# The 512-column products of a two-block network take their columns in a reversed, alternating order

## What is computed

```python
proj = jnp.einsum('btd,de->bte', hn, w_in)                # first block: q, k, v, gate
gate, up = jnp.split(jnp.einsum('btd,de->bte', hn, w_in), 2, axis=-1)
... = jnp.einsum('btf,fd->btd', jax.nn.silu(gate) * up, w_out)
gate = jax.nn.sigmoid(jnp.einsum('btd,de->bte', rmsnorm(h, ple_norm[i]), ple_w_gate[i]))
proj = jnp.einsum('bsd,de->bse', h, w_in[l])              # second block
br_a = jnp.einsum('bsc,cd->bsd', y_a, w_proj_mlstm[l])
out = jnp.einsum('bsd,de->bse', merged, w_out[l])
```

## Time and profile before

| | us |
|---|---|
| median of 3 runs | 2201.73 |
| lowest, highest | 2200.83, 2202.91 |
| profiled execution | 2200.2 |
| its span, first to last instruction | 2198.5 |
| PE busy | 2188.7 |
| DVE busy | 1574.8 |
| ACT busy | 1082.1 |

### The profile page before, as it was taken

One profiled execution on the slowest core, in us unless ns is written; L12 is line 12 of the kernel. 1 busy time (PEld: TensorE's weight loads), 2 busy tenths in 40 slices (PEclk: granted clock), 3 DMA queues, 4 the chain that ended last, 5 costly groups with the idle time before them and its releaser, 6 DMA issues.

```text
span 2198.5 us, 27733 instructions
## 1 busy us (share of the span) xinstructions
PE 2188.7 (100%) x9954; PEld 1819.9 (83%) x9954; DVE 1574.8 (72%) x2395; ACT 1082.1 (49%) x1369; POOL 19.8 (1%) x41
## 2 busy tenths in 40 slices
PE   9999999999999999999999999999999999999998
PEld 8888888888888888888888888888888888888887
DVE  6887888877776457777778846889455559645875
ACT  5564554544444334444446545555445555443443
POOL 0000000000000000000000000000000000000000
PEclk9999999999999999999999999999999999999999
DMA  9654566666666666666666656666665556666663
GB/s 281 182 163 122 179 196 189 200 192 195 194 193 192 192 195 191 196 191 194 186 217 198 200 152 191 183 199 181 201 176 171 171 162 205 196 195 211 191 192 114
DMA packets 282925, 413.96 MB, mean 188 GB/s; under 512 B 21071, under 2 KB 145883, under 8 KB 282299
## 3 DMA queue, kind: packets, MB, share of 16 engines
q1 hardware_dynamic: 281806, 408.55, 61.9%
q10 hardware_dynamic: 1008, 3.94, 0.5%
HBM read 410.33 MB, written 2.10 MB: 188 GB/s over the span
## 4 chain that ended last, share of the span: by engine, by line
PE 99%; issue 0%; DMA 0%; DVE 0%; ACT 0%; DVEq 0%; POOLq 0%; POOL 0%; SPq 0%; ACTq 0%
PE acc L1314 31%; PE acc L1316 31%; PE acc L1315 31%; PE mx L1494 1%; PE mx L1535 0%; PE tp L1362 0%; DMA H<-in_x 0%; PE tp L1508 0%; PE tp L1507 0%; PE tp L1509 0%; PE mx L1291 0%; PE mx L1293 0%; PE mx L1292 0%; PE mx L1472 0%; PE tp L1552 0%
## 5 line engine op out<-in xcount | busy, mean ns | idle before, releaser
L1686 DVE TENSOR_TENSOR w_lo<-raw,w_hi 128x1024 fp32r<-128x1024 f32 (+1 forms) x769 | 934.9, 1219 | 524.5 <-ACT w_hi L801 520.7
L801 ACT CAST w_hi<-raw 128x1024 fp32r<-128x1024 f32 (+1 forms) x769 | 803.0, 1046 | 913.9 <-PE acc L1316 897.0
L1314 PE MATMUL acc<-w_hi,xa_hi 128*128 128x512 f32 x2228 | 874.8, 393 | 0.0
L1316 PE MATMUL acc<-w_hi,xa_lo 128*128 128x512 f32 x2228 | 867.4, 389 | 0.0
L1315 PE MATMUL acc<-w_lo,xa_hi 128*128 128x512 f32 x2228 | 867.2, 389 | 0.0
L1316 PEld LDWEIGHTS acc<-w_hi,xa_lo 128*128 128x128 f32 x2228 | 418.2, 188 | 87.8
L1314 PEld LDWEIGHTS acc<-w_hi,xa_hi 128*128 128x128 f32 x2228 | 418.5, 188 | 84.8
L1315 PEld LDWEIGHTS acc<-w_lo,xa_hi 128*128 128x128 f32 x2228 | 418.6, 188 | 84.2
L1314 PE MATMUL acc<-w_hi,xb_hi 128*128 128x512 f32 x384 | 149.6, 390 | 0.0
L1316 PE MATMUL acc<-w_hi,xb_lo 128*128 128x512 f32 x384 | 149.4, 389 | 0.0
L1315 PE MATMUL acc<-w_lo,xb_hi 128*128 128x512 f32 x384 | 149.4, 389 | 0.0
(11 more groups left out here) (313 smaller groups left out, 1240.4 us busy)
## 6 DMA issues: line engine op xcount, KB each, us to landing
raw<-in_w_in SPq DMA_DIRECT2D x192, 512.0 KB, 3.8
raw<-in_ffn_w_in SPq DMA_DIRECT2D x352, 256.0 KB, 2.9
raw<-in_gla_w_in SPq DMA_DIRECT2D x95, 512.0 KB, 4.0
raw<-in_ffn_w_out SPq DMA_DIRECT2D x88, 512.0 KB, 3.7
raw<-in_w_in SPq DMA_DIRECT2D x128, 256.0 KB, 3.0
raw<-in_gla_w_out SPq DMA_DIRECT2D x32, 512.0 KB, 4.1
raw<-in_ple_w_gate SPq DMA_DIRECT2D x32, 512.0 KB, 4.0
raw<-in_w_proj_mlstm SPq DMA_DIRECT2D x32, 512.0 KB, 3.7
```

The source lines that it names most:

```text
L801: nc.scalar.copy(w_hi[:, hl, 0:kc * job.w], raw[:, slot, 0:kc * job.w]).then_inc(hi_ready, 1)
L1314: nc.tensor.matmul(a[t][:, 0:w], xh, hi, start=first, stop=False)
L1316: ins = nc.tensor.matmul(a[t][:, 0:w], xl, hi, start=False, stop=last)
L1686: nc.vector.tensor_tensor(w_lo[:, hl, 0:kc * job.w], raw[:, slot, 0:kc * job.w], w_hi[:, hl, 0:kc * job.w].bitcast(F32), ALU.subtract) \
```

## The change

The three matmuls of `product` take rearranged views of their moving operand and of their output. The new helper splits the 512 columns into two halves h of 32 blocks b of eight columns c, and goes through them with b from last to first outermost, then the two halves, then c from last to first. The opening granules (`opening_product`), the narrow products, the embedding product and the job `pool` keep their views.

```diff
                     for t in range(2) if only is None else (only,):
                         xh = xt_part(job, 0, k)[:, t * P:(t + 1) * P]
                         xl = xt_part(job, 1, k)[:, t * P:(t + 1) * P]
-                        nc.tensor.matmul(a[t][:, 0:w], xh, hi, start=first, stop=False)
-                        nc.tensor.matmul(a[t][:, 0:w], xh, lo, start=False, stop=False)
-                        ins = nc.tensor.matmul(a[t][:, 0:w], xl, hi, start=False, stop=last)
+                        to, high, low = streamed(a[t][:, 0:w]), streamed(hi), streamed(lo)
+                        nc.tensor.matmul(to, xh, high, start=first, stop=False)
+                        nc.tensor.matmul(to, xh, low, start=False, stop=False)
+                        ins = nc.tensor.matmul(to, xl, high, start=False, stop=last)
                     if kk == kc - 1 and only != 0:
                         ins.then_inc(consumed, 1)
                     elif last and only == 0:
                         ins.then_inc(half_done, 1)
+
+            def streamed(tile):
+
+                return tile.rearrange("p (h b c) -> p b h c", h=2, c=8)[:, ::-1, :, ::-1]
```

## The result

The changed kernel takes 2419.41 us (median of 4 runs, 2418.88 to 2421.15) against 2201.28 us for the kernel before; the ratio is 1.0991, 95% interval 1.0972 to 1.1011. It is slower by 218.1 us, 24.0 ns for each of the 9084 changed matmuls. The forecast was no change; the measured time lies in the span of rival A (2270 to 2443 us), near its upper end.

The account below looks back on a forecast made before the run. PE was taken to bound the kernel throughout; instructions 0 plus stream 0 left profiled execution at 2200.2 us, and 1.5 us for the median gave 2201.7 us. Likeliest range 2197 to 2206 us, eight in ten 2197 to 2443 us.

Parts of the forecast that it names:

- rival A: Inside each of the 9084 matmuls, every run change costs a little at full pace: +68 to +241 us, 2270 to 2443 us; chance 0.17.
- The bound: PE busy in 100% of the span, waiting only 2.6 us, so a slower matmul costs its whole increase; 9084 matmuls at 226.7 ns.
- Part (1): Instructions on all queues: none added, removed or moved, no wait, semaphore or transfer changed; cost 0.
- part (2): Column streaming in the changed matmuls: bounds from -134 to +1926 us, 0 taken from the nearest earlier row.
- the row at l = 8: Gated scores, F32, ascending runs of eight alternating between two planes: 101 ns a matmul, no penalty seen; nearest evidence for 0.
- l = 1: Gated scores with read and output stepping by two columns: eight matmuls in 0.82 us against 0.81, taken as no cost.
- l = 2: Gated scores in alternating runs of two columns: 0.87 us against 0.81 for eight matmuls, 7.5 ns per 128 columns.
- 0.117 ns per run: Possible price of each run change in a changed matmul, from the scores' runs of two: 7.5 ns a matmul, +68 us.
- l = 4: Gated scores in alternating runs of four columns: 0.81 us for eight matmuls, no cost where a price per run predicted 0.03 us.
- Rival B: Changed matmuls' stream falls to half rate through descending pairs or broken output: +1926 us, 4128 us; chance 0.17.
- Rival C: A gain in the changed matmuls as their time beside streaming shrinks: down to 2068 us at the utmost; chance 0.03.
- the 14.7 ns beside the streaming: Part of each changed matmul's 226.7 ns pace beyond 212 ns for 512 columns; its whole removal would give -134 us.

## Why the prediction was wrong

**The bound** was read rightly. PE sets the time throughout, nothing is hidden, and 9084 times the change of pace is the result: +24.0 ns gave +218 us. The other way it is so only in the main: 9120 x -10.9 ns is -99 us, of which 89 came, since PE then waits a little for DVE.

**Part (1)** held: the instruction counts are equal, the clock's row stayed, and the unchanged groups kept their durations but for the 36 opening products. The dearest group of these has a mean of 457 ns instead of 417, but 417 in the kernel that only reads in the new order and takes the same time, so this isn't the order's doing, and it is under 2 us in all.

**The failed step is the choice of 0 in part (2)**: the row at l = 8 of the earlier trace rows, ascending and at 0.828 ns a column, was taken for the changed matmuls at 0.414 ns a column. The prediction had named this limit ("a penalty that brings a column from 0.414 up to 0.828 ns could hide there") and then chosen by likeness of shape. The alternating ascending kernel is that very shape at the full pace, and costs 16.4 ns a matmul, (212 + 16.4) / 512 = 0.446 ns a column: far below 0.828. That such a price hides under the slow pace of an F32 pass fits the read at a step of two: nothing in the F32 rows (l = 1), and 451 ns in F32R, (451 - 14.7) / 512 = 0.852 ns a column. But it stays an argument, and one row speaks against it: alternating runs of two did show at l = 2, though in F32R they have a pace of 333 ns, (333 - 14.7) / 512 = 0.62 ns a column, also below 0.828. Shown is that the row at l = 8 doesn't carry over to the full pace; why isn't. The second half of the choice, that a reversed run touches the same words and is free, failed too: 6.5 ns for the plain reversal, and 9 ns of duration for the descending blocks on top of the alternation (416 against 407).

**Rival A** has the place (inside each matmul, PE's other groups unchanged) and, by its upper bound of 26.5 ns, nearly the size, but not the mechanism: neither of its prices describes the rows. 0.117 ns per run gives 3.7 ns for runs of sixteen, which cost 13.2. One column's time per run does give 13.2 ns there (32 x 0.414), but 53 ns for runs of four, which cost 23.2, and 26.5 ns for 64 runs, which cost 16.4 when they alternate in ascending order and 6.4 when the blocks go backwards over the whole tile. That its bound lay close to 24.0 ns is chance. I had given it 0.17 because l = 4 and l = 8 showed nothing at the slow pace.

**Rival B** is out: the moving operand's descending order costs 6.5 ns, not 212, and the output's order nothing. The sentence weighed there, that "any non-contiguous AP slows matmuls significantly" (the Trainium skill, PSUM — Partial Sum Buffer, Specifications), doesn't hold for this output: 2200.44 against 2200.31 us. For the read, the Trainium skill's Advanced Engine Details and Errata (SBUF Cachelines) has full performance as long as at least two accesses hit a 16-byte line. The runs here disagree both ways: each run of eight fills two such lines, and the alternating kernel is 6.8% slower all the same; two columns in turn, 256 apart, never hit a line twice in a row, and are faster than plain order.

**Rival C**, a gain from the 14.7 ns beside the streaming, didn't come with this order, and I was wrong that nothing could touch them: with two columns in turn the pace is 215.8 ns, 10.9 of the 14.7 gone.

**What stays open** is the mechanism of the fetch. Shown is: it is the read of the moving operand; it costs from some run length between 32 and 64 columns downwards when far halves alternate; the distance is of little weight; no DMA and no work of ACT or DVE beside it is needed for the price; any reversal or block order of 4, 8 or 16 columns over the whole tile costs the same 6 to 7 ns; swapping neighbouring blocks of eight, ascending inside, costs much more, 43 ns of duration. That the read alone matters is shown for the order of the change, and with runs of two (508 and 502 ns) nearly so; for the other orders that were tried on both sides it is assumed. No law that I tried covers these rows, and whether the weight load, which runs beside each matmul, takes part wasn't tried.

## What to carry to other kernels

A price read from a slower instruction bounds nothing below that instruction's own time per element: take the row at the pace of the matmul that is changed, or keep the whole gap in the range and in the chances. Where PE is the bound and its matmuls are back to back, the order in which the moving operand is read is worth a trial of its own: read and write are separate questions, each a one-line experiment, and one kernel with a different order in each job prices a dozen orders at once. A read of two columns in turn, with the columns put back in place by evacuations that cost the same at a step of two, made this kernel 4.1% faster.

## What was not expected of the hardware

- Plain ascending order is not the fastest for a 512-column F32R moving operand: a pace of 226.7 ns, against about 216 ns for two columns in turn at distances from 4 to 256 columns, forwards or backwards, and 217 ns for the same eight columns again and again.
- Four columns in turn have a pace of 283 ns and eight in turn 487 ns. The even and then the odd columns at a step of two have 451 ns, twice the plain pace.
- Plain order begun one column late lasts 399 ns instead of 389, begun eight late 395.
- The output takes runs of eight, reversed and alternating between the halves of a bank, at no price, and DVE and ACT read a bank at a step of two columns as fast as at a step of one (DVE 682 against 681 ns, ACT 681 against 680).
